# A Toeplitz bias band for windowed attention: read back from replicated rows in device memory, where it was read reversed and turned round by matmuls

## The reference

```python
def rel_bias(dist, t5_table):
    b = t5_table.astype(jnp.float32)[t5_bucket(dist)]
    return jnp.transpose(b, (2, 0, 1)).reshape(N_KV_HEADS, GQA_GROUP, *dist.shape)
...
    qi = jnp.arange(ATTN_BLOCK)[:, None]
    kj = jnp.arange(2 * ATTN_BLOCK)[None, :]
    dist = qi + ATTN_BLOCK - kj
    s = s + rel_bias(dist, t5_table)
    valid = ((dist >= 0) & (dist <= WINDOW))[None] & (key_pos >= 0)
    p = sink_softmax(s, valid[None, :, None, None], sinks).astype(v.dtype)
```

## Time and profile before

| | us |
|---|---|
| median of 3 runs | 1410.02 |
| lowest and highest run | 1409.33 and 1414.19 |
| the profiled execution | 1408.94 |
| its span, first to last instruction | 1407.2 |
| PE busy | 1291.8 |
| DVE busy | 461.1 |
| ACT busy | 316.7 |
| POOL busy | 71.5 |

### The profile page before, as it was taken

How to read it: one execution, slowest core, us unless ns; L and a number is a source line. 1 busy time by engine, 2 the same in 40 slices (tenths; PEclk the granted TensorE clock), 3 DMA queues, 4 the chain that set the end, 5 groups by cost and what they waited for, 6 DMA issues and landing times.

```text
span 1407.2 us, 21314 instructions
## 1 busy us (share of the span) xinstructions
PE 1291.8 (92%) x8359; PEld 649.1 (46%) x8359; DVE 461.1 (33%) x1061; ACT 316.7 (23%) x563; POOL 71.5 (5%) x62
## 2 busy tenths in 40 slices
PE   6999768889797999999999999999999999999997
PEld 4887457867585333333333333333333333333333
DVE  2056533333635322332233222332223322233223
ACT  3014632200102221222122211222112221122212
POOL 0000701223200000000000000000000000000000
PEclk9999988999898999999999999999999999999999
DMA  9965130047513699999999999999999999999994
GB/s 368 318 232 212 38 120 2 3 153 271 213 60 120 246 416 429 428 428 428 428 428 428 428 428 428 428 428 428 429 428 429 428 429 428 429 428 429 428 428 173
DMA packets 55362, 465.44 MB, mean 331 GB/s; under 512 B 4989, under 2 KB 7297, under 8 KB 29706
## 3 DMA queue, kind: packets, MB, share of 16 engines
q1 hardware_dynamic: 53370, 461.09, 79.0%
q0 software_dynamic: 1408, 3.63, 0.8%
q10 hardware_dynamic: 544, 0.13, 0.0%
HBM read 462.36 MB, written 3.52 MB: 331 GB/s over the span
## 4 chain that ended last, share of the span: by engine, by line
PE 49%; DMA 42%; DVE 5%; ACT 2%; issue 1%; SPq 0%; POOL 0%; DVEq 0%; ACTq 0%
DMA ring<-in_w 40%; PE ps L1207 16%; PE ps L768 7%; PE ps L1233 5%; PE ps L1161 2%; PE ps L1119 2%; DMA ring<-in_w_mod 2%; PE ps L1098 2%; PE ps L1185 2%; PE ps L1072 1%; PE ps L777 1%; PE ps L745 1%; PE ps L1215 1%; PE ps L996 1%; DMA ring<-in_w_in 1%
## 5 line engine op out<-in xcount | busy, mean ns | idle before, releaser
L1207 PE MATMUL ps<-ring,PT 128*64 128x512 f32 x2048 | 449.8, 593 | 21.8 <-DMA ring<-in_w 21.0
L1207 PEld LDWEIGHTS ps<-ring,PT 128*64 128x64 f32 x2048 | 144.8, 137 | 320.8 <-issue 271.9
L1654 DVE TENSOR_TENSOR SQ<-ps,SQ 128x528 f32<-128x528 f32 x132 | 84.2, 700 | 626.4 <-PE ps L1185 626.4
L1233 PE MATMUL ps<-ring,PT 128*64 128x512 f32 x1024 | 226.8, 595 | 0.0
L1233 PEld LDWEIGHTS ps<-ring,PT 128*64 128x64 f32 x1024 | 70.5, 137 | 133.4 <-issue 133.4
L655 ACT COPY SG<-ps 128x512 f32<-128x512 f32 x64 | 34.4, 589 | 405.6 <-PE ps L1207 405.6
L768 PE MATMUL ps<-HT,ring 128*128 128x264 f32 x448 | 107.6, 401 | 1.9 <-DMA ring<-in_w_in 1.9
L768 PEld LDWEIGHTS ps<-HT,ring 128*128 128x128 f32 x448 | 87.8, 198 | 20.1 <-issue 2.6
L1161 PE MATMUL ps<-XR,PT 128*64 128x512 f32 x396 | 94.2, 611 | 1.6 <-DVE PT L1626 1.6
L1185 PE MATMUL ps<-PT 64*128 64x264 f32 x528 | 76.3, 408 | 0.8 <-ACT PT L668 0.8
L1185 PEld LDWEIGHTS ps<-PT 64*128 64x128 f32 x528 | 45.3, 185 | 44.9 <-issue 27.6
(11 more groups left out here) (375 smaller groups left out, 1130.5 us busy)
## 6 DMA issues: line engine op xcount, KB each, us to landing
ring<-in_w SPq DMA_DIRECT2D x192, 2048.0 KB, 20.9
ring<-in_w_mod SPq DMA_DIRECT2D x12, 2048.0 KB, 14.4
ring<-in_w_in SPq DMA_DIRECT2D x9, 2048.0 KB, 8.9
ring<-in_w_o SPq DMA_DIRECT2D x2, 2048.0 KB, 16.8
ring<-in_w_pa SPq DMA_DIRECT2D x1, 2048.0 KB, 7.8
ring<-in_w_pb SPq DMA_DIRECT2D x1, 2048.0 KB, 19.7
XR<-in_x_prompt SPq DMA_DIRECT2D x2, 512.0 KB
SG<-bias_by_distance POOLq DMA_DIRECT2D x1, 1024.0 KB, 9.0
```

The costliest lines, as they stand in the source:

```text
L1207: last = mm(ps[64 * lin:64 * lin + 64, 2 + hh, :], XG[:, k % 4, k // 4, :], slot_tile(c)[:, k % 2, lin * FE + hh * 512:lin * FE + hh * 512 ...
L1233: last = mm(ps[64 * hh:64 * hh + 64, 4, :], AC[:, f, :], slot_tile(c)[:, f % 4, hh * 512:hh * 512 + 512], start=(f == 0), stop=(f == NF - 1))
L1654: v.tensor_tensor(YA[:, p::4, :], ps[:, bank:bank + 2, 0:T], YA[:, p::4, :], ALU.add).then_inc(sem["comb_used"], 1)
```

## The change

The DRAM tensor becomes 8 x 128 x 384: each head's row is written 128 times, from the same 8 partitions, by a source pattern with a step of zero. The read starts at element 127 and steps 383 numbers from one copy to the next, where the copies are 384 apart, so that partition p reads its copy from element 127 - p on. That is the band in its right order, and it goes straight into BM. The matmuls with `K_REV`, their copies on ACT, the tile `HK` and the semaphores `bm_done` and `bm_evac` are gone. DVE waits for the read itself (`ld_bm`) ahead of its first use of BM. PE waits for `kc_evac` ahead of the scores.

```diff
-        HK = view(SG, 0, HQ, 2 * P)
...
-        ext_d = nc.dram_tensor("bias_by_distance", [HQ, 384], F32, kind="Internal")
+        ext_d = nc.dram_tensor("bias_by_distance", [HQ, P, 384], F32, kind="Internal")
...
-            pool.dma_start(ext_d.ap(), ext[0:HQ, :]).then_inc(sem["ext_out"], 16)
+            pool.dma_start(ext_d.ap(), ext[0:HQ, :].unsqueeze(1).broadcast_to([HQ, P, 384])).then_inc(sem["ext_out"], 16)
             pool.wait_ge(sem["ext_out"], 16)
-            band = bass.AP(ext_d, 0, [[1, P], [384, HQ], [1, 2 * P]])
-            pool.dma_start(HK, band).then_inc(sem["ld_hk"], 16)
+            band = bass.AP(ext_d, P - 1, [[384 - 1, P], [384 * P, HQ], [1, 2 * P]])
+            pool.dma_start(BM[:, :].rearrange("p (a b) -> p a b", b=2 * P), band).then_inc(sem["ld_bm"], 16)
...
-            for i in range(4):
-                act.wait_ge(sem["bm_done"], i + 1)
-                act.copy(BM[:, i * 512:i * 512 + 512], ps[:, [6, 7, 4, 5][i], :]).then_inc(sem["bm_evac"], 1)
-
...
-            pe.wait_ge(sem["ld_hk"], 16)
-            HKf = HK.rearrange("p a b -> p (a b)")
-            for i in range(4):
-                if i == 2:
-                    pe.wait_ge(sem["kc_evac"], 1)
-                mm(ps[:, [6, 7, 4, 5][i], :], cst[:, K_REV:K_REV + P], HKf[:, i * 512:i * 512 + 512],
-                   start=True, stop=True).then_inc(sem["bm_done"], 1)
-
...
             pe.wait_ge(sem["qs_evac"], 1)
-            pe.wait_ge(sem["bm_evac"], 4)
+            pe.wait_ge(sem["kc_evac"], 1)
...
             dve.wait_ge(sem["decays"], 4)
-            dve.wait_ge(sem["bm_evac"], 4)
             dve.wait_ge(sem["qs_done"], 1)
...
+            dve.wait_ge(sem["ld_bm"], 16)
             BMv = BM[:, :].rearrange("p (a b) -> p a b", b=2 * P)
             dve.wait_ge(sem["ld_sink"], 32)
```

## The result

The change makes the kernel slower. Seven runs after have a median of 1422.89 us (1418.49 to 1424.69), seven runs before 1409.33 us. The ratio is 1.0089, with a 95% interval of 1.0071 to 1.0108. The forecast was 1407.6 with a range from 1404.5 to 1413.5. The profiled execution after took 1423.95 us, its span 1422.2 us.

A forecast was written before the change was run, and what follows sets the result against it. The prediction took waits for expert weights as 40% of the chain, with time gained ahead of the expert loop on PE's path counting in full. The 2.44 us step, other costs nothing, gave 1410.02 - 2.44 = 1407.6 us; range 1404.5 to 1413.5.

The forecast's parts named there:

- The slow write: Replicated 1.57 MB write from 8 partitions: bounded at 13.5 to 47 us, about 30 taken, covered by other work; cost nothing.
- the stall among the rivals: Rival: write clogs the weight loads, PE stands 15.4 us ahead of projection block 4, 1423 us; chance 0.16.
- The bytes: Weight loads beside the write: block 4's load delayed 5.7 us, inside its 8.7 us to spare; cost nothing.
- the sum stays as it is: By the skill's pages the write lands near 102 us (28.5 us estimated), leaving the forecast unchanged.
- the rest of a shift counts in full: Expert loop: time gained or lost ahead of it on PE's path reaches the end in full.
- The 2.44 us: First attention group: of 3.0 us from PE, 0.6 is lost in the first wait; each operation one POOL operation earlier.
- the group moves in steps of POOL's operations: First attention group: DVE operations with two SBUF inputs stand until POOL's current operation ends, a step of 2.44 us.
- when L1405 is ready: DVE, first group: ready at 148.8 us, 1.3 us before POOL's L393 ends at 150.09.
- the filler group: PE's work ahead of L886: ends near 151.4 us, or 155.3 at twice its duration, ahead of 157.9.
- no gain: Rival: L1405 misses 150.09 us, so the first wait swallows all; 1410.0 us; chance 0.12.
- The scores did move up: PE, first attention group: scores start at 146.5 us instead of 149.47, a shift of 3.0 us.
- ACT's copies were worth nothing by themselves: ACT: four copies go, their time worth only what PE and DVE waited for it, already counted.

The follow-up runs named there:

- experiment 1: Kernel before the change with only the replicated 1.57 MB write from the same 8 partitions added, into a tensor nobody reads: 1425.38 us, ratio 1.0119.
- experiment 2: Changed kernel with the same 1024 rows written from 128 partitions, each written 8 times, after one more matmul: 1407.09 us, ratio 1.0001.
- experiment 3: Changed kernel with the source rows on partitions 0, 4, 8 to 28 in place of 0 to 7: 1408.65 us, ratio 0.9994.
- experiment 6: Changed kernel with 12 KB written from the 8 partitions, then copied 128 times inside device memory by a second DMA: 1408.25 us, ratio 0.9986.
- experiment 9: Changed kernel writing from 128 partitions, plus three unread matmuls filling PE's gap ahead of `Qs`: 1409.39 us, ratio 1.0001.
- experiment 10: Changed kernel writing from 128 partitions, with three unread matmuls in PE's gap and POOL's RWKV preparation held back until the fourth attention group: 1398.33 us, ratio 0.9949.
- experiment 4: Changed kernel with the replicated write issued by ACT in place of POOL: 1417.59 us, ratio 1.0069.

## Why the prediction was wrong

**The slow write, priced at nothing.** This step failed. I had the write's duration in my bounds: 13.5 to 47 us, and about 30 as the value taken; it took 35.9. I also had the stall among the rivals, at 15.4 us and 1423, against 14.7 us and a median of 1422.89. What I got wrong is the step "The bytes": I charged the load only for the write's bytes, at the 117 GB/s of the band's read, and found 5.7 us of delay inside a slack of 8.7. (The 12.6 us in that sum should be 13.2 by my own start at 73.6, which makes 5.9 us and changes nothing.) But a slow write doesn't slow the loads by its bytes. It slows them by the time for which it keeps its engines, and a load that is cut over all 16 engines has landed only when its part on the slow ones has. The rows of the queues show that: the write held 45 to 47% of the engines' time, and SP's loads moved 1.11 MB from 96 to 102 us, as much as half of block 4's, which landed only at 121.4. The row of 56 KB from 8 partitions showed the pace; I called it a low guess and it was the nearest row. Experiments 1, 2, 3 and 6 show the cause from four sides: the write alone does it, and does it from another queue too, and the same bytes from elsewhere don't.

The rival's working was not right in its detail either. It had 33 GB/s, and the loads getting as much as the write on the shared engines; in the trace the write ran at 45 GB/s and the engines moved 57 in all from 90 to 96 us, so that the loads got next to nothing there. Nor did block 4's load land during the write, but 12.8 us after its end, behind the load of `w_mod` (113.1) and beside the band's read. That these errors cancel is luck. The two passages of the Trainium skill that I named speak of the write itself (page "SBUF — State Buffer", section "Door 1: The DMA port swizzle", and page "DMA: Bandwidth & Descriptors", section "Rules for kernel authors"). The trace agrees with them on the engines, of which the write held just under half, and has it slower than my estimate, 35.9 us against 28.5. Neither passage says what the write does to others, and I took "the sum stays as it is" from that silence.

**The path from the stall to the end.** From 106.77 to 121.47 are 14.7 us. Block 4 then took 16.06 us instead of 14.44, with the clock at its lower level behind the wait (granted 0.50 from 108 to 120 us and 0.61 from 120 to 126, 1.00 before the change), so PE was 16.3 us late. At the loop it is 480.18 - 465.95 = 14.2 us late. Nearly all of the 2 us between came back late: at L1098 (L1085 after) PE is still 370.78 - 354.59 = 16.2 us behind. Just ahead of the loop the granted clock was 0.80 (445 to 480 us) where it was 0.76 (430 to 466) before the change; whether that is the reason was not followed further. That the rest of a shift counts in full held: the loop's last wait starts 14.4 us later, and the span is 15.0 us longer.

**The 2.44 us.** The mechanism was right: the group moves in steps of POOL's operations. The step that failed is when L1405 is ready. I had it 148.8 - 143.54 = 5.3 us behind POOL's start, with 1.3 us in hand. It came at 166.59 - 159.85 = 6.74. The 1.5 us are three parts (the times not shown above are from the same timelines): ACT's `kvrow_evac` came 0.53 us later against POOL's start (161.66 - 159.85 = 1.81 in place of 1.28); `Qs` took 1.48 us in place of 1.02; and from the scores to L1389 it took 1.37 us in place of 0.86. The last two are PE's clock at its lower level behind a gap of 3.26 us, as experiments 9 and 10 show. The reversing matmuls had filled the first part of that gap. I had weighed this clock for the filler group, where it costs nothing, and called `Qs` and the scores too short for it to matter. The rival "no gain" put the point of decision in the right place. How near it was shows in two versions of the change in which nothing was done about the clock: with 16 copies and with the write from ACT the gap was 2.90 and 3.01 us, `Qs` ran in 1.06 us, and they head the table below.

All kernels in which POOL runs as before, in the order in which L1405's operation is ready behind POOL's start, from the starts in their timelines:

| kernel | ready | group ends |
|---|---|---|
| 16 copies | 6.03 | 14.38 |
| write from ACT | 6.25 | 14.39 |
| copies in device memory | 6.63 | 14.43 |
| filler matmuls | 6.63 | 14.43 |
| the change | 6.74 | 16.80 |
| 8 partitions apart | 6.89 | 16.81 |
| from 128 partitions | 7.11 | 16.81 |
| before | 8.23 | 16.81 |
| the write alone | 10.30 | 17.23 |

POOL's second large operation starts at 6.64. Of the eight that are ready within 8.3 us, four end at one place and four at the other, 2.4 us apart, with nothing between. (With the write alone the group is so late that its last operation comes behind POOL's last large one and isn't held.) By this table, 1.6 us could have been taken from the path in the kernel before without any effect.

**What held.** The scores did move up against the work ahead of them, the filler group was covered, ACT's copies were worth nothing by themselves, and neither DVE nor ACT waited for the bias: the read was issued at 108.8 and took 9.3 us, wanted at 165.

**What stays open.** Why the loads fare better beside the write from ACT's queue (a stall of 8.8 us against 14.9) was not tried further. SP's issue of block 4's load took 5.48 us in the change and 0.37 us in experiments 1 and 4, where the stall was 11.3 and 8.8 us, so a part may lie in SP's own queue. Whether the loads' packets for partitions 0 to 7 also waited at the same ports as the write's was not separated from the wait for its engines. The number of copies at which the stall begins was not looked for: 16 are free and 128 are not. A read with a negative step between partitions, which would need no copies at all, was not tried on the chip either.

## What to carry to other kernels

Price a DMA by how long it keeps its engines, and look up which load shares them and when it is wanted. A broadcast out of 8 neighbouring partitions was the slowest of the sources tried, and spreading the same rows over partitions four apart took the stall away. When one engine waits for another's operations one by one, its time moves in steps: look how far the next step is before counting a saving, and see whether the other engine's work can simply come later. That last edit, one line, made the kernel before faster by itself (1403.82 against 1409.35 us); the change with the wide source alone did not (1407.09 against 1409.05, ratio 1.0001), and both together gave 1400.91.

## What the runs showed of the hardware

- 1.57 MB in rows of 1536 bytes took 35.9 us out of partitions 0 to 7, 15.1 us out of partitions 0, 4 to 28, and 10.9 us out of 128 partitions, each beside the same weight loads. From a row of 12 KB in device memory it took 9.0 us.
- The write out of partitions 0 to 7 took 45 to 47% of the 16 engines' time at 45 GB/s. The weight loads on SP's queue moved 0.06 MB beside it from 90 to 96 us and 1.11 MB from 96 to 102, and the 2 MB load issued at 90.17 landed after 31.3 us in place of 7.7.
- A DVE TENSOR_SCALAR with one SBUF tensor waited for POOL's operation too (2.21 us, experiments 6 and 9), as the TENSOR_TENSOR operations with two did. A TENSOR_REDUCE that started under a POOL operation took its usual 0.69 us, and so did the TENSOR_TENSOR that reads one input from PSUM. RECIPROCAL never started under one.
- A gap of 3.26 us on PE was followed by small matmuls that ran at the lower clock for a part or all of their time (1.44 to 1.88 us in six kernels, against 1.06), and 2.74 us of matmuls in that gap kept the clock up. Behind gaps of 2.90 and 3.01 us they took 1.06.
